# Two transformer layers on one core: attention heads turned by VectorE and exchanged through DRAM instead of transposed by TensorE, and the last product finished half by half

## The chip, the cores and the metric

The kernel runs on one core of a Trainium2 chip. The metric is the device time of one execution in microseconds (us). A difference of 0.2% (5.3 us) is about the least that a measurement of this kernel can tell from no change.

## The reference, cut to what matters

Two layers are computed one after the other on a sequence of 256 tokens and a width of 2048, all in float32.

- The first layer normalizes `x`, multiplies it with `w_in` and gets the input of two attentions of eight heads each. In MLA the queries (8 heads of 128 + 64 columns) and the keys and values (8 heads of 128 + 128 columns) come from two more products with low-rank latents; the 64 last columns of a query and one common key of 64 columns are rotated (rope). In FoX queries, keys and values (8 heads of 128) come from `w_in` directly, and a decay is added to the scores. Both are gated, then comes `w_out`, a norm and the residual.
- The second layer is a gated feed-forward block (width 5632), a mixer (three groups of four dilated attention heads of 128 columns, whose queries and keys are partly rotated, a spatial gating branch, and two gates), and a second feed-forward block. It ends with an RMS norm of the rows, times `final_norm_2`:

```python
x = x + 0.5 * swiglu(rmsnorm(x, ffn2_norm), w_gate, w_up, w_down)
return rmsnorm(x, final_norm)
```

## The kernel before, in words

**Products.** Tokens are the rows of a result: two halves of 128 tokens lie on the 128 partitions. A product streams weights in *groups* of 256 rows (two tiles of 128) by 512 columns. SyncE (SP) loads a group into one of four slots (`raw`, L322 to L334) once VectorE is done with what was there. ScalarE rounds it to `whi` (`split_hi`, L852 to L867), VectorE makes the rest `wlo = raw - whi` (`split_lo`, L1217 to L1226), both three groups ahead of TensorE (`AHEAD = 3`). TensorE multiplies (`groups`, L466 to L500): for each group 12 matmuls of 512 columns, four of `hi x whi`, four of `lo x whi`, four of `hi x wlo`. The activations are the stationary operand, transposed (`act_hi`, `act_lo`, `lat_hi`, ...). The groups that sum into one pair of accumulators (`acc`, two pairs in turn) are a *unit*: 8 groups for an input of 2048 rows, 3 for the query latent, 2 for the key-value latent, 22 for the last product of a feed-forward block. ScalarE takes half 0 of a finished unit and VectorE half 1 (`copy_out`, L936 and L1322); TensorE may start a unit only when the one before the last was taken (`acc_free`).

**Order of the work.** Everything else stands between groups, by lists written by hand. Units 3 to 5 make the queries `q`, units 6 to 9 the keys and values `kv`; VectorE rotates `q` at the first two of the latter (L1499 to L1512), its output going to `q_rope`, and the common key at the third. Then come six units of FoX queries, keys and values, four of gates and four of `w_out`. `n` counts the groups from the first FoX unit on. `MLA_STEPS` (L99) and `FOX_STEPS` (L101) say at which `n` a step of a head comes: `heads`, `scores`, `probs`, `values`. `MIX_STEPS` (L104) does the same in the mixer from its u and vs units on.

**A head before.** In the step `heads` TensorE transposes the head's queries and keys, four blocks of 128 by 128, into a PSUM bank (`job`, L502 to L511; called by `mla_step` L597, `fox_step` L615, `mix_step` L629); MLA adds two blocks of `q_rope` with every second head. ScalarE copies the bank to `qkT1` or `qkT2` (`job_out`, L954), VectorE copies the rotated part (`qrT`). In the step `scores` (L560 to L572) TensorE multiplies them: queries of the second half by 256 keys, of the first half by 128. In MLA a second pair of matmuls adds the rotated part. VectorE masks the scores and takes the row maximum, ScalarE the exponential; `probs` transposes three blocks of the probabilities, `values` multiplies with V.

**Feed-forward blocks.** Each of 11 chunks of the hidden activations is turned without TensorE: VectorE transposes it in squares of 32 by 32 (L1708, `h_turned`), and GpSimd moves it to DRAM (L428) and back in four pieces, one per 32 partitions (L431, `h_back`), by which the squares change places. Splitting it into `h_hi` and `h_lo` undoes the rest of the order (L907, L1280).

**The end.** VectorE adds the last unit to the residual (L1401) for both halves at once, takes the statistics of both (L1294), aggregates them (L1300), and with ScalarE's square root gets the row scale (L1313). Then ScalarE scales half 0 and VectorE half 1 of the four chunks of 512 columns (L1200, L1902); the gain of the last chunk is multiplied in between (L1668). SP sends each chunk, 512 KB, once both halves are ready (L395 to L399).

Of the kernel before, what the change touches and what calls it, by code (L numbers as in the profile page):

```python
# [32 lines left out]
P = 128  # L33
# [61 lines left out]
FFN1_READY = 3 + 2 * CHUNKS  # L95
FFN2_READY = FFN1_READY + FF_CHUNKS + CHUNKS + 1 + 3 + 2 * CHUNKS
# [7 lines left out]
MIX_STEPS = [(8 * h + d, step, h, g) for h in range(PER_GROUP)  # L104
             for d, step, g in ((0, "heads", 0), (1, "scores", 0), (1, "heads", 1), (2, "scores", 1),
                                (2, "heads", 2), (3, "scores", 2), (5, "probs", 0), (5, "probs", 1),
                                (6, "probs", 2), (7, "values", 0))]
# [49 lines left out]
def build(nc, x, positions, w_in, w_uq, w_ukv, b_forget, w_out, g_post, ffn1_w_gate_2, ffn1_w_up_2,  # L157
# [3 lines left out]
    with ctx:  # L161
# [36 lines left out]
        s1, pt1, qkT1 = lat[:, 0, 0:384], lat[:, 0, 384:768], lat[:, 0, 768:768 + 2 * SEQ]  # L198
        qrT, top = place_at("qrT", [P, SEQ], F32, top)
# [18 lines left out]
        rope_tmp = o_sb[:, 0, 0:4 * HEADS * ROPE // 2].rearrange("p (a h d) -> p a h d", a=4, h=HEADS)  # L218

# [21 lines left out]
        wsp_raw = u2[:, :, :].rearrange("p h n -> p (h n)")[:, 0:SG_W].rearrange("p (g s) -> p g s", g=SG_GROUPS)  # L241
        att_hi, top = place_at("att_hi", [P, PER_GROUP, SEQ], F32R, top)
# [12 lines left out]
        mix_tmp2 = pt2[:, :, :].rearrange("p g n -> p (g n)")  # L255


        h_dram = nc.dram_tensor("h_dram", (P, QUADS, TURN), F32, kind="Internal").ap()
# [16 lines left out]
        group_used = sem("group_used")  # L275
        acc_free = [sem(f"acc_free{i}") for i in range(2)]
# [4 lines left out]
        h_left, h_landed = sem("h_left"), sem("h_landed")  # L281
# [22 lines left out]
        pool_step = sem("pool_step")  # L304
        out_ready, out_sent = [sem(f"out_ready{h}") for h in range(HALVES)], sem("out_sent")
# [13 lines left out]
        def _(sp):  # L319
# [75 lines left out]
            for c in range(CHUNKS):  # L395
                for half in range(HALVES):
                    sp.wait_ge(out_ready[half], c + 1)
                sp.dma_start(out[:, c * W:(c + 1) * W].rearrange("(h p) n -> p h n", p=P),
                             xres[:, :, c * W:(c + 1) * W]).then_inc(out_sent, 16)  # L399
            sp.wait_ge(out_sent, 16 * CHUNKS)  # L400
# [6 lines left out]
        def _(pool):  # L407
# [3 lines left out]

            pool.wait_ge(forget_v, 5)
# [9 lines left out]
            blocks = h_dram.rearrange("(a j) q r -> q j a r", a=QUADS)  # L422

            def exchange_h_chunks(ready, done):

                for i in range(FF_CHUNKS):
                    pool.wait_ge(chunk_ready, ready + i + 1)
                    pool.dma_start(h_dram, h_turned[:]).then_inc(h_left, 16)  # L428
                    pool.wait_ge(h_left, 16 * (done + i + 1))
                    for quad in range(QUADS):  # L430
                        pool.dma_start(h_back[quad * QUAD:(quad + 1) * QUAD], blocks[quad]).then_inc(h_landed, 16)  # L431

            pool.wait_ge(group_used, after_first)
            exchange_h_chunks(FFN1_READY, 0)

# [4 lines left out]
            pool.dma_start(ln_b, sg_ln_b_2[:, :].partition_broadcast(P)).then_inc(ln_in, 16)  # L440
            pool.wait_ge(ln_in, 32)
# [12 lines left out]
            pool.wait_ge(group_used, after_mixer)  # L454
            exchange_h_chunks(FFN2_READY, FF_CHUNKS)
            pool.wait_ge(chunk_split, CHUNKS + FFN2_READY + FF_CHUNKS)
# [6 lines left out]
        def _(pe):  # L463
            at = Place()

            def groups(count, hi, lo, width=W, opened_by_part=False):  # L466
# [9 lines left out]
                for j in range(count):  # L476
# [9 lines left out]
                    pe.wait_ge(hi_ready, at.target("group", 1))  # L486
                    for t in range(TILES):
                        for half in range(HALVES):
                            product(hi, whi, t, half, start=first and t == 0)
# [38 lines left out]
            def h_turns():  # L528

                at.n["ready"] += 1  # L530
                at.n["chunk"] += 1

# [27 lines left out]
            def scores(terms_of):  # L560
# [4 lines left out]
                for cols, tok, keys in ((slice(0, 256), slice(P, 2 * P), slice(0, SEQ)),  # L565
                                        (slice(256, 384), slice(0, P), slice(0, P))):
                    terms = terms_of(tok, keys)
                    for n, (left, right) in enumerate(terms):
                        last = nc.tensor.matmul(s_ps[:, cols], left, right, start=(n == 0),  # L569
                                                stop=(n == len(terms) - 1), skip_group_check=True)  # L570
# [26 lines left out]
            def mla_step(step, h):  # L597
                if step == "heads":
                    job([(P, slice(half * P, half * P + P), q[:, half, h * QK:h * QK + NOPE]) for half in range(HALVES)]
                        + [(P, slice(SEQ + half * P, SEQ + half * P + P), kv[:, half, h * 2 * P:h * 2 * P + P])  # L600
                           for half in range(HALVES)])
                    if h % 2 == 0:
                        job([(P, slice(half * P, half * P + P), q_rope[:, half, h * ROPE:(h + 2) * ROPE])
                             for half in range(HALVES)])
# [10 lines left out]
            def fox_step(step, h):  # L615
                if step == "heads":
                    job([(P, slice(part * SEQ + half * P, part * SEQ + half * P + P),
                          fox[:, half, part * FOX + h * P:part * FOX + (h + 1) * P])
                         for part in range(2) for half in range(HALVES)])
                elif step == "scores":  # L620
                    transposed()
                    scores(lambda tok, keys: [(qkT1[:, tok], qkT1[:, SEQ + keys.start:SEQ + keys.stop])])
# [6 lines left out]
            def mix_step(step, h, g):  # L629
                c = (g * PER_GROUP + h) * P  # L630
                if step == "heads":
                    job([(P, slice(part * SEQ + half * P, part * SEQ + half * P + P),
                          qk2[:, half, part * ATT_W + c:part * ATT_W + c + P])
                         for part in range(2) for half in range(HALVES)])
                elif step == "scores":
                    transposed()
                    scores(lambda tok, keys: [(qkT2[:, tok], qkT2[:, SEQ + keys.start:SEQ + keys.stop])])
# [96 lines left out]
            def ffn(first_one):  # L734
# [15 lines left out]
                for i in at.loop(pe, FF_CHUNKS - 1, dict(group=2 * G_D, unit=2, chunk=1, ready=1)):  # L750
# [96 lines left out]

        @block.scalar
        def _(act):
            at = Place()  # L850

            def split_hi(n):  # L852

# [353 lines left out]
        def _(dve):  # L1207
# [545 lines left out]
            for j in groups(G_D):  # L1753
                if j == 7:
                    copy_out(qk2, slice(W, 2 * W), "mix")
# [215 lines left out]
```

## Time and profile before

| | us |
|---|---|
| median of 3 runs (2656.45 to 2657.12) | 2656.97 |
| the profiled execution's own time | 2656.65 |
| its span | 2654.8 |
| TensorE busy in the span | 2637.2 |
| VectorE busy | 1456.0 |
| ScalarE busy | 1192.1 |
| GpSimd busy | 88.8 |

The mean granted clock of TensorE is 0.998 of full speed. The span is the time from the first to the last record of the profiled execution; the execution's own time is 1.9 us longer. A busy time is the sum over an engine's instructions without overlaps; matmuls are pipelined, so the start of one to the start of the next is shorter than the duration that is printed for one.

### The profile page before, as it was taken

What the parts mean: (1) busy time and instruction counts of PE and PEld (TensorE: products, weight loads), DVE (VectorE), ACT (ScalarE), POOL (GpSimd) and SP (SyncE); (2) the same over time, 40 slices, a digit from 0 to 9 for tenths busy, and PEclk for the clock granted to TensorE, in tenths of its full rate; (3) what the DMA queues carried; (4) which work ended last, traced back from release to release, by engine and by line L of the source; (5) the groups of instructions that cost most, each with busy time, mean ns of one, the idle gap of its engine ahead of it and who ended that gap; (6) DMA issues with size and microseconds to landing.
All of it is one profiled execution on the core that took longest, in us unless ns stands there. A gap on an engine that the chain in (4) does not pass through costs nothing.

```text
span 2654.8 us, 32291 instructions
## 1 busy us (share of the span) xinstructions
PE 2637.2 (99%) x12033; PEld 2193.1 (83%) x12033; DVE 1456.0 (55%) x1594; ACT 1192.1 (45%) x1362; POOL 88.8 (3%) x137
## 2 busy tenths in 40 slices
PE   9999999999999999999999999999999999999998
PEld 8888888788888888888888888888888888888886
DVE  7755565755555555555446655555655555555554
ACT  5544554444444444444444554444444444444333
POOL 0000000000000000000000300000000000000000
PEclk9999999999999999999999999999999999999999
DMA  7655656577777775657666446665567767777654
GB/s 217 195 159 169 194 160 192 157 223 213 221 217 218 218 216 191 191 191 232 195 191 182 145 145 188 191 191 191 185 207 207 227 205 222 213 221 228 192 189 151
DMA packets 266658, 520.37 MB, mean 196 GB/s; under 512 B 19435, under 2 KB 22345, under 8 KB 266313
## 3 DMA queue, kind: packets, MB, share of 16 engines
q1 hardware_dynamic: 257456, 489.88, 61.0%
q0 software_dynamic: 8608, 29.02, 3.6%
q8 instruction: 59, 0.97, 0.1%
q10 hardware_dynamic: 504, 0.26, 0.0%
q14 instruction: 31, 0.25, 0.0%
HBM read 505.45 MB, written 13.64 MB: 196 GB/s over the span
## 4 chain that ended last, share of the span: by engine, by line
PE 99%; DVE 1%; ACT 0%; issue 0%; DVEq 0%; POOL 0%; ACTq 0%; POOLq 0%
PE acc L482 95%; PE tr L509 2%; PE s_ps L569 1%; PE o_ps L592 1%; PE s_ps L545 0%; PE tr L805 0%; DVE act_lo L1257 0%; DVE stats L1294 0%; ACT act_hi L896 0%; DVE xres L1660 0%; DVE u L1839 0%; DVE xres L1650 0%; ACT lat L958 0%; DVE xres L1902 0%; DVE xres L1401 0%
## 5 line engine op out<-in xcount | busy, mean ns | idle before, releaser
L1225 DVE TENSOR_TENSOR wlo<-raw,whi 128x1024 fp32r<-128x1024 f32 x929 | 1133.0, 1224 | 1040.6 <-ACT whi L866 1033.8
L866 ACT ACTIVATE whi<-raw 128x1024 fp32r<-128x1024 f32 x929 | 978.9, 1057 | 1121.1 <-PE acc L482 1112.8
L482 PE MATMUL acc<-whi,act_hi 128*128 128x512 f32 (+1 forms) x2560 | 693.5, 393 | 0.4 <-ACT whi L866 0.4
L482 PE MATMUL acc<-whi,act_lo 128*128 128x512 f32 (+1 forms) x2560 | 682.7, 388 | 0.0
L482 PE MATMUL acc<-wlo,act_hi 128*128 128x512 f32 (+1 forms) x2560 | 682.3, 388 | 0.0
L482 PEld LDWEIGHTS acc<-whi,act_lo 128*128 128x128 f32 x2560 | 479.6, 188 | 100.5
L482 PEld LDWEIGHTS acc<-wlo,act_hi 128*128 128x128 f32 x2560 | 479.6, 188 | 99.5
L482 PEld LDWEIGHTS acc<-whi,act_hi 128*128 128x128 f32 x2560 | 471.9, 188 | 91.7 <-issue 0.6
L482 PE MATMUL acc<-whi,h_hi 128*128 128x512 f32 x704 | 188.4, 389 | 0.0
L482 PE MATMUL acc<-wlo,h_hi 128*128 128x512 f32 x704 | 188.2, 389 | 0.0
L482 PE MATMUL acc<-whi,h_lo 128*128 128x512 f32 x704 | 188.2, 389 | 0.0
L482 PEld LDWEIGHTS acc<-whi,h_lo 128*128 128x128 f32 x704 | 132.1, 188 | 27.5
L482 PEld LDWEIGHTS acc<-wlo,h_hi 128*128 128x128 f32 x704 | 132.1, 188 | 27.5
L482 PEld LDWEIGHTS acc<-whi,h_hi 128*128 128x128 f32 x704 | 131.9, 188 | 27.2
L428 POOL DMA_DIRECT2D h_dram<-h_turned x22 | 12.4, 562 | 1476.8 <-DVE h_turned L1708 1476.8
L431 POOL DMA_DIRECT2D h_back<-h_dram x88 | 48.1, 554 | 66.8 <-DMA h_dram<-h_turned 65.4
L948 ACT ACTIVATE g_sb<-acc,rs 128x512 f32<-128x512 f32 x44 | 27.9, 686 | 33.2 <-PE acc L482 33.2
L966 ACT ACTIVATE lat<-lat,soft 128x128 f32<-128x128 f32 (+1 forms) x32 | 14.3, 449 | 57.8 <-DVE soft L1383 57.8
L1257 DVE SCALAR_TENSOR_TENSOR act_lo<-tr,gains,act_hi 128x256 fp32r<-128x256 f32 x64 | 26.6, 477 | 24.7 <-ACT act_hi L896 24.7
L958 ACT ACTIVATE lat<-tr 128x512 f32<-128x512 f32 (+1 forms) x32 | 17.4, 544 | 48.1 <-PE tr L509 48.1
L896 ACT ACTIVATE act_hi<-tr,gains 128x256 fp32r<-128x256 f32 x64 | 25.2, 474 | 30.4 <-PE tr L509 30.4
L1704 DVE SCALAR_TENSOR_TENSOR h_sb<-acc,rs,g_sb 128x512 f32<-128x512 f32 x44 | 31.0, 746 | 12.0 <-PE acc L482 12.0
(221 smaller groups left out, 1343.8 us busy)
## 6 DMA issues: line engine op xcount, KB each, us to landing
raw<-in_w_in SPq DMA_DIRECT2D x280, 512.0 KB, 3.8
raw<-in_ffn_w_gate SPq DMA_DIRECT2D x176, 512.0 KB, 4.4
raw<-in_ffn_w_up SPq DMA_DIRECT2D x176, 512.0 KB, 4.0
raw<-in_ffn_w_down SPq DMA_DIRECT2D x176, 512.0 KB, 4.7
raw<-in_w_out SPq DMA_DIRECT2D x64, 512.0 KB, 4.3
raw<-in_w_sg_out SPq DMA_DIRECT2D x24, 512.0 KB, 4.2
h_dram<-h_turned POOLq DMA_DIRECT2D x22, 512.0 KB, 3.2
h_back<-h_dram POOLq DMA_DIRECT2D x88, 128.0 KB, 5.3
```

Of the source, the lines that this page charges most:

```text
L431: pool.dma_start(h_back[quad * QUAD:(quad + 1) * QUAD], blocks[quad]).then_inc(h_landed, 16)
L482: return nc.tensor.matmul(pair[:, half, 0:width], left[:, k, half * P:(half + 1) * P], right[:, slot, t, 0:width], start=start, stop=stop, ...
L509: last = nc.tensor.transpose(tr[bank][0:rows, cols], src, ident[0:src.shape[0], 0:src.shape[0]])
L569: last = nc.tensor.matmul(s_ps[:, cols], left, right, start=(n == 0), stop=(n == len(terms) - 1), skip_group_check=True)
L592: last = nc.tensor.matmul(o_ps[:, qb * P:(qb + 1) * P], left, right, start=(n == 0), stop=(n == len(terms) - 1), skip_group_check=True)
L866: nc.scalar.activation(whi[:, slot, :, 0:width], raw[:, slot, :, 0:width], ACT.Copy).then_inc(hi_ready, 1)
L896: last = nc.scalar.activation(hi[:, tile + k, :], tr[bank][:, t * SEQ:(t + 1) * SEQ], ACT.Copy, scale=gains[:, gain + k:gain + k + 1])
L948: last = nc.scalar.activation(dest[:, half, :], a[:, half, :], func, scale=scaled(norm, half))
L958: nc.scalar.activation(dest, tr[bank][0:rows, src_cols], ACT.Copy).then_inc(tr_free[bank], 1)
L1225: nc.vector.tensor_tensor(wlo[:, slot, :, 0:width], raw[:, slot, :, 0:width], whi[:, slot, :, 0:width].bitcast(F32), ALU.subtract).then_in ...
L1257: last = nc.vector.scalar_tensor_tensor(lo[:, tile + k, :], tr[bank][:, t * SEQ:(t + 1) * SEQ], gains[:, gain + k:gain + k + 1], hi[:, til ...
L1704: last = nc.vector.scalar_tensor_tensor(h_sb[:, half, :], a[:, half, :], scaled(norm, half), g_sb[:, half, :], ALU.mult, ALU.mult)
```

## The change

- *Heads.* The step `heads` is gone from all three lists, and with it the transposes of queries and keys by TensorE and the copies `qkT1`, `qkT2`, `qrT`. VectorE turns four heads (128 x 1024 numbers) at a time in squares of 32, in two instructions (`turn_heads`), and GpSimd exchanges them through one of two DRAM buffers, as it did for the feed-forward chunks (`exchange`). There are 15 new exchanges: MLA 5 (queries of heads 0 to 3, of heads 4 to 7, rotated parts, keys 0 to 3, keys 4 to 7), FoX 4, mixer 6. The order in DRAM is such that a head lies in the landed tile at every eighth number: token, then head, then half. The scores read it there (`head_rows`).
- *Places.* MLA's turns come at the first groups of key-value units 0, 1 and 2 and of the first FoX unit; FoX's and the mixer's behind `copy_out` of the units that make queries and keys. In the mixer the rotation, two big ones before, is done there too, unit by unit. `MLA_STEPS` start at n = 8 with four groups for a head (at n = 0 with five before); both end at n = 39.
- *Waits.* VectorE waits for earlier turned tiles to have left (`turn_left`) before it overwrites them; GpSimd waits for the exchange before (`turn_landed`); TensorE waits for the exchanges that a head needs (`landed`).
- *Last group.* TensorE does half 0 of the last group, then half 1, six matmuls each, and signals after each. VectorE adds and takes the statistics of half 0 while TensorE works on half 1. The gain and the scale of the last chunk are one instruction for each half, both on VectorE; the output goes out in eight transfers of 256 KB.

```diff
-MLA_STEPS = [(5 * h + d, step, h) for h in range(HEADS)
-             for d, step in ((0, "heads"), (1, "scores"), (3, "probs"), (4, "values"))]
+EX_MLA, EX_FOX, EX_FFN1 = 0, 5, 9
+EX_MIX = EX_FFN1 + FF_CHUNKS
+EX_FFN2 = EX_MIX + 6
+MLA_STEPS = [(8 + 4 * h + d, step, h) for h in range(HEADS)
+             for d, step in ((0, "scores"), (2, "probs"), (3, "values"))]
 FOX_STEPS = [(48 + 4 * h + d, step, h) for h in range(HEADS)
-             for d, step in ((4, "values"), (0, "heads"), (1, "scores"), (3, "probs"))]
+             for d, step in ((4, "values"), (1, "scores"), (3, "probs"))]
...
+            def exchange(n, left, back):
+                pool.wait_ge(turned, n + 1)
+                pool.dma_start(turn_dram[n % 2], left.rearrange("p (q r) -> p q r", q=QUADS)).then_inc(turn_left, 16)
+                pool.wait_ge(turn_left, 16 * (n + 1))
+                if n:
+                    pool.wait_ge(turn_landed, 16 * QUADS * n)
+                for quad in range(QUADS):
+                    pool.dma_start(back[quad * QUAD:(quad + 1) * QUAD].rearrange("p (a r) -> p a r", a=QUADS),
+                                   blocks[n % 2][quad]).then_inc(turn_landed, 16)
+            for i in range(5):
+                exchange(EX_MLA + i, mla_turned[i], mla_back[i])
+            for i in range(4):
+                exchange(EX_FOX + i, fox_turned, fox_back[i])
...
 # TensorE, groups()
+                    if ends_by_half and final:
+                        pe.wait_ge(lo_ready, at.target("group", 1))
+                        for half in range(HALVES):
+                            for t in range(TILES):
+                                product(hi, whi, t, half)
+                            for t in range(TILES):
+                                product(lo, whi, t, half)
+                            for t in range(TILES):
+                                last = product(hi, wlo, t, half, stop=t == TILES - 1)
+                            last.then_inc((half_used, group_used)[half], 1)
...
+            def head_rows(back, head, tok):
+                rows = back.rearrange("p (t k h) -> p k h t", k=4, h=HALVES)[:, head]
+                if tok.stop - tok.start == P:
+                    return rows[:, tok.start // P]
+                return rows
...
             def mla_step(step, h):
-                if step == "heads":
-                    job([...])
-                elif step == "scores":
-                    transposed()
-                    scores(lambda tok, keys: [(qkT1[:, tok], qkT1[:, SEQ + keys.start:SEQ + keys.stop]),
-                                              (qrT[:, tok], (krT_odd if h % 2 else krT_even)[:, keys])])
+                if step == "scores":
+                    landed(EX_MLA + 3 + h // 4)
+                    scores(lambda tok, keys: [
+                        (head_rows(mla_back[h // 4], h % 4, tok), head_rows(mla_back[3 + h // 4], h % 4, keys)),
+                        (head_rows(mla_back[2], h // 2, tok), (krT_odd if h % 2 else krT_even)[:, keys])])
...
 # VectorE
+            def turn_heads(dest, source):
+                squares = dest.rearrange("p (q i k h) -> p h k q i", q=QUADS, k=4, h=HALVES)
+                for half in range(HALVES):
+                    last = nc.vector.transpose(squares[:, half], source[:, half].rearrange("p k (q j) -> p k q j", j=QUAD))
+                last.then_inc(turned, 1)
...
+            def add_last_residual(c, factor):
+                a, free = pair()
+                cols = slice(c * W, (c + 1) * W)
+                for half in range(HALVES):
+                    if half == 0:
+                        dve.wait_ge(half_used, 1)
+                    else:
+                        unit_ready()
+                    settled(nc.vector.scalar_tensor_tensor(xres[:, half, cols], a[:, half, :], factor, xres[:, half, cols],
+                                                           ALU.mult, ALU.add))
+                    settled(row_stats(stats, c, xres[:, half, cols], half))
+                    if half == 0:
+                        settled(aggregate("final", stats, 4, 0))
...
             for c in range(4):
                 for j in groups(KVR // P // TILES):
                     if j == 0 and c < 2:
                         if c == 0:
                             unit_out(4)
                             unit_out(5)
+                            for i in range(2):
+                                turn_heads(mla_turned[i], q[...][:, :, 4 * i:4 * i + 4, 0:NOPE])
...
+                        if c == 1:
+                            dve.wait_ge(rope_ready, 2)
+                            turn_heads(mla_turned[2], q_rope.rearrange("p a (k d) -> p a k d", d=P))
                     if j == 0 and c == 2:
+                        unit_out(6)
+                        unit_out(7)
+                        turn_keys(0)
...
             for c in range(6):
                 for j in groups(G_D):
+                    if n == 0:
+                        unit_out(8)
+                        unit_out(9)
+                        turn_keys(1)
                     attention_at(n)
                     n += 1
                     if j == 7:
+                        dve.wait_ge(turn_left, 16 * min(5, 2 * (c // 2 + 1)))
                         copy_out(fox, slice(c * W, (c + 1) * W), "pre")
+                        if c < 4:
+                            unit_out(at.n["unit"])
+                            dve.wait_ge(turn_left, 16 * (EX_FOX + c))
+                            turn_heads(fox_turned, fox[:, :, c * W:(c + 1) * W].rearrange("p a (k d) -> p a k d", d=P))
...
+            def heads_out(c):
+                copy_out(qk2, cols, "mix")
+                unit_out(at.n["unit"])
+                rotate(rows[:, :, :, 0:16], rows[:, :, :, 16:32], ...)
+                dve.wait_ge(rope_ready, rotated[0])
+                dve.wait_ge(turn_left, 16 * (EX_MIX + c))
+                turn_heads(mix_turned[:], rows)
...
+            dve.wait_ge(final_gained, CHUNKS - 1)
+            for c in range(CHUNKS - 1):
                 cols = slice(c * W, (c + 1) * W)
                 nc.vector.tensor_scalar(xres[:, 1, cols], xres[:, 1, cols], scaled("final", 1), None,
                                         ALU.mult).then_inc(out_ready[1], 1)
+            cols = slice((CHUNKS - 1) * W, CHUNKS * W)
+            for half in reversed(range(HALVES)):
+                nc.vector.scalar_tensor_tensor(xres[:, half, cols], xres[:, half, cols], scaled("final", half),
+                                               gfinal[:, cols], ALU.mult, ALU.mult).then_inc((out_last, out_ready[1])[half], 1)
```

## Rows read from the trace of the kernel before

**Rows 1.** The page: busy time of TensorE, and the chain that ended last.

```profile
PE 2637.2 (99%) x12033; PEld 2193.1 (83%) x12033; DVE 1456.0 (55%) x1594; ACT 1192.1 (45%) x1362; POOL 88.8 (3%) x137
...
PE 99%; DVE 1%; ACT 0%; issue 0%; DVEq 0%; POOL 0%; ACTq 0%; POOLq 0%
```

**Rows 2.** Waits of TensorE: total us, times, longest; the largest of four.

```profile
PE tr L509 <- DVE xres L1660: 2.7, 2, 1.7
```

**Rows 3.** Groups of instructions by form: TensorE's transposes of heads (busy us, mean ns).

```profile
L509 PE MATMUL tr<-fix,qk 128*128 128x128 f32 x48 | 7.2, 272 | 0.0
...
L509 PE MATMUL tr<-fix,o_sb 128*128 128x128 f32 x40 | 6.3, 277 | 0.4
...
L509 PE MATMUL tr<-fix,fox 128*128 128x128 f32 x32 | 4.8, 272 | 0.0
...
L509 PE MATMUL tr<-fix,q 128*128 128x128 f32 x16 | 3.0, 271 | 0.0
```

**Rows 4.** Timeline of TensorE around a FoX head and an MLA head: start us, us.

```profile
276.57 1.07 PE L482 MATMUL acc<-wlo,act_hi 128*128 128x512 f32 x4
...
278.84 1.08 PE L482 MATMUL acc<-whi,act_lo 128*128 128x512 f32 x4
279.75 1.07 PE L482 MATMUL acc<-wlo,act_hi 128*128 128x512 f32 x4
...
282.24 1.08 PE L482 MATMUL acc<-whi,act_lo 128*128 128x512 f32 x4
...
120.56 1.08 PE L482 MATMUL acc<-wlo,act_hi 128*128 128x512 f32 x4
...
123.06 1.08 PE L482 MATMUL acc<-whi,act_lo 128*128 128x512 f32 x4
```

**Rows 5.** Groups by form: the matmuls of the scores and their weight loads.

```profile
L569 PE MATMUL s_ps<-lat 128*128 128x256 f32 x32 | 9.5, 377 | 0.0
...
L569 PE MATMUL s_ps<-lat 128*128 128x128 f32 x32 | 6.1, 274 | 0.0
...
L569 PEld LDWEIGHTS s_ps<-lat 128*128 128x128 f32 x64 | 12.1, 188 | 2.1
```

**Rows 6.** VectorE's square transpose by form, and the timeline of the key-value units.

```profile
L1708 DVE STREAM_TRANSPOSE h_turned<-h_sb 128x1024 f32<-128x1024 f32 x22 | 27.4, 1245 | 0.7
...
98.43 1.23 DVE L1225 TENSOR_TENSOR wlo<-raw,whi 128x1024 fp32r<-128x1024 f32 x1 [0.97 <-ACT whi L866]
...
108.29 0.74 DVE L1326 TENSOR_SCALAR kv<-acc,rs 128x512 f32<-128x512 f32 x1
...
112.82 1.07 PE L482 MATMUL acc<-whi,lat_hi 128*128 128x512 f32 x4
```

**Rows 7.** The page, DMA issues: KB each, median us from issue to landing.

```profile
h_dram<-h_turned POOLq DMA_DIRECT2D x22, 512.0 KB, 3.2
h_back<-h_dram POOLq DMA_DIRECT2D x88, 128.0 KB, 5.3
```

**Rows 8.** The end: a group of VectorE by form, the timeline, and one window.

```profile
L1704 DVE SCALAR_TENSOR_TENSOR h_sb<-acc,rs,g_sb 128x512 f32<-128x512 f32 x44 | 31.0, 746 | 12.0 <-PE acc L482 12.0
...
2641.97 1.07 PE L482 MATMUL acc<-wlo,h_hi 128*128 128x512 f32 x4
2643.15 1.23 DVE L1401 SCALAR_TENSOR_TENSOR xres<-acc,xres 128x1024 f32<-128x1024 f32 x1 [8.57 <-PE acc L482]
2644.41 1.29 DVE L1294 BATCH_NORM_STATS2 stats<-xres 128x6 f32<-128x512 f32 x2
2645.73 0.39 DVE L1300 BATCH_NORM_AGGREGATE moments<-stats 128x2 f32<-128x24 f32 x2
...
2646.98 0.49 DVE L1902 TENSOR_SCALAR xres<-xres,rs 128x512 f32<-128x512 f32 x1
...
2647.72 3.13 SPq L398 DMA_DIRECT2D out<-xres  x4
...
2649.00:2650.00 1.00, 0.00 (x0) 0.00 (x0) 0.85 (x3) 0.53 (x1) 0.00 (x0) 0.50 0.98 381
```

More of the change, by code:

```diff
@@ L420, in _ @@
             pool.dma_start(gpost[:], g_post[:, :].partition_broadcast(P)).then_inc(gpost_in, 16)
[L422 to L434, printed above, removed]
+            flat_h = [t[:].rearrange("p q r -> p (q r)") for t in (h_turned, h_back)]
+            for i in range(FF_CHUNKS):
+                exchange(EX_FFN1 + i, *flat_h)
             pool.wait_ge(group_used, after_ffn1)
@@ L440, in _ @@
             pool.dma_start(ln_b, sg_ln_b_2[:, :].partition_broadcast(P)).then_inc(ln_in, 16)
+            for i in range(6):
+                exchange(EX_MIX + i, mix_turned[:], mix_back[i])
             pool.wait_ge(ln_in, 32)
@@ L568, in scores @@
                     for n, (left, right) in enumerate(terms):
-                        last = nc.tensor.matmul(s_ps[:, cols], left, right, start=(n == 0),
+                        out_cols = s_ps[:, cols]
+                        if len(right.shape) == 3:
+                            out_cols = out_cols.rearrange("p (h t) -> p h t", h=HALVES)
+                        last = nc.tensor.matmul(out_cols, left, right, start=(n == 0),
                                                 stop=(n == len(terms) - 1), skip_group_check=True)
@@ L615, in fox_step @@
             def fox_step(step, h):
[L616 to L622, printed above, removed]
+                if step == "scores":
+                    landed(EX_FOX + 3)
+                    scores(lambda tok, keys: [(head_rows(fox_back[h // 4], h % 4, tok),
+                                               head_rows(fox_back[2 + h // 4], h % 4, keys))])
                 elif step == "probs":
@@ L629, in mix_step @@
             def mix_step(step, h, g):
[L630 to L637, printed above, removed]
+                if step == "scores":
+                    landed(EX_MIX + 5)
+                    scores(lambda tok, keys: [(head_rows(mix_back[g], h, tok),
+                                               head_rows(mix_back[GROUPS_M + g], h, keys))])
                 elif step == "probs":
@@ L749, in ffn @@
                     pass
-                for i in at.loop(pe, FF_CHUNKS - 1, dict(group=2 * G_D, unit=2, chunk=1, ready=1)):
+                for i in at.loop(pe, FF_CHUNKS - 1, dict(group=2 * G_D, unit=2, chunk=1)):
                     for j in groups(G_D, act_hi, act_lo):
@@ L1096, in ffn @@
                     pass
-                for i in at.loop(act, FF_CHUNKS - 1, dict(group=2 * G_D, unit=2, chunk=1, ready=1, turn=1)):
+                at.n["turn"] = EX_FFN1 if first_one else EX_FFN2
+                for i in at.loop(act, FF_CHUNKS - 1, dict(group=2 * G_D, unit=2, chunk=1, turn=1)):
                     for j in groups(G_D):
@@ L1714, in ffn @@
                         gated()
-                for i in at.loop(dve, FF_CHUNKS - 1, dict(group=2 * G_D, unit=2, chunk=1, chunk_job=2, ready=1, turn=1)):
+                at.n["turn"] = EX_FFN1 if first_one else EX_FFN2
+                for i in at.loop(dve, FF_CHUNKS - 1, dict(group=2 * G_D, unit=2, chunk=1, chunk_job=2, turn=1)):
                     for j in groups(G_D):
```

179 lines of the change are left out of this document (88 added, 91 removed).

## The prediction

> **What bounds the kernel now.** I read the page first: TensorE is busy 2637.2 of 2654.8 us and makes up 99% of the chain that ended last, while VectorE has 55% and ScalarE 45% [rows 1]. Then its waits: the longest in total is 2.7 us, for two residual chunks [rows 2]. So TensorE's queue is full from start to end. An instruction taken out of it is a gain of its whole pace, as long as the two engines that prepare weights stay ahead; what the change puts on VectorE and the queues is free until it uses up that lead. Only the last 12 us belong to others: from the end of the last matmul on, VectorE, ScalarE and the output transfers follow one another [rows 8].
>
> **Transposes taken out.** The form rows show 48 transposes for the mixer, 32 for FoX, 16 for MLA's queries, as many for its keys [rows 3]. Of the 40 that read `o_sb`, 8 are of `q_rope` (four jobs of two). That is 120 in 28 jobs: 24 of four, and four in which two more are added. Their printed mean of 272 ns is latency; the pace is what counts. A set of four plain matmuls follows the one before after 279.75 - 278.84 = 0.91 us [rows 4], so a group takes 2.72 us. Around a FoX job, from the `wlo` set before to the `act_lo` set behind it are 278.84 - 276.57 = 2.27 us, where two sets take 1.82: the job of four costs 0.45 us. In MLA with six it is 123.06 - 120.56 - 1.82 = 0.68 us [rows 4]. Sum: 24 x 0.45 + 4 x 0.68 = **13.5 us** less. The copies of the banks by ScalarE and VectorE go too, at no gain: no wait of TensorE names them [rows 2].
>
> **Scores read at a stride of eight numbers.** Both operands now come from the landed tile, 32 bytes from one number to the next; the common rotated key stays packed. No row of before has a stationary or moving operand with such a step, so I bound it. A score's four passes cost 282.24 - 279.75 - 1.82 = 0.67 us in FoX [rows 4]. By form, the 256-column pass takes 377 and the 128-column pass 274 ns, so 128 columns more cost 0.103 us and a pass runs at about 0.206 or 0.103 us [rows 5]. The weight load in front of it hides behind the pass before; it takes at most the pace of a transpose, 0.45 / 4 = 0.113 us. Lower bound: nothing, since these passes take a column in 0.80 ns where the fp32r matmuls take 512 in 0.91 / 4 = 0.227 us, 0.44 ns each [rows 4, 5]. The fetch of a number therefore has almost twice the time that packed operands need. Upper bound, every strided read at half the pace: 28 pairs of head operands (8 MLA, 8 FoX, 12 mixer) x 2 x (0.206 + 0.103) = 17.3 us, and for MLA's rotated term, where only the load is strided, its 0.226 us stands against the passes of 0.206 and 0.103: 8 x 2 x (0.02 + 0.123) = 2.3 us. Together 19.6 us. Below nothing is excluded, for the matmuls stay the same in number and columns. I take **0**, because the nearest rows are those of the same passes, which leave this spare time per number; the upper end is kept.
>
> The Trainium skill speaks against the change here. "Advanced Engine Details and Errata", section "SBUF Cachelines", says that lines have 16 bytes, that at least two hits on one are needed to cover the memory's latency, and that a different line for each access costs a penalty. By that rule each number of these operands is such a miss, and the sum would come out near the upper bound. No row of before shows it either way.
>
> **VectorE and its lead.** A square transpose of 1024 numbers takes 1.245 us [rows 6]; in two halves I put 1.35 us. Fifteen are 20 us of an engine with 1200 us to spare, but they fall in bursts. In the FoX and mixer units a burst (copy, rotation, turn) is 2 to 4 us in 21.8, against a lead of three groups, 8.2 us: nothing. The tight place is the key-value units, of two groups (5.4 us) each. There VectorE takes its half of key-value unit 1 at 108.29, done at 109.03, and TensorE needs that accumulator at 112.82 [rows 6]: 3.8 us of room. Three turns are put ahead of it, 4.05 us, of which VectorE's idle gaps between 98.43 and 108.29 swallow about 0.3 to 0.6. I take **0.3 us** more. Queued behind these turns on VectorE are `wlo` of the next groups (they keep about 2 us) and SP's loads. Upper bound, if writing at a stride doubles the turns: 3 x 2.7 - 3.8 - 0.6 = 3.7 us there, and about 4.5 us by the next unit, whose copy has four turns ahead of it. Below nothing: excluded, since no work of VectorE's that TensorE waits for is removed here.
>
> **Exchanges.** One takes 3.2 us out and 5.3 back [rows 7], 8.5 if nothing overlaps. The first turn of MLA ends near 98.43 + 1.23 + 1.35 = 101.0 us; four exchanges in a row end by 135. The first FoX unit starts 5.9 us behind 112.82, at 118.7, and head 0's scores stand eight groups later, at 140.5: 5 us of room. VectorE's wait for the fifth to have left, at the end of the same unit, comes due when it has (135 + 3.2). FoX's and the mixer's have 22 us each and whole units before the scores. Cost 0; upper bound, if the exchanges take 11.5 us each under the weights' own traffic, 6 us. GpSimd has nothing else queued behind them that is due.
>
> **The end.** Half 0 of the last group is done six matmuls early, 6 x 0.227 = 1.36 us. VectorE's add can start at 2643.15 - 1.36 = 2641.8. With 0.746 us for an add of 512 numbers, 1.29 / 2 for its statistics, 0.39 / 2 for the aggregate and 0.03 between them [rows 8], half 0 is through at 2643.5 and half 1 at 2645.2, where both were at 2646.12: 0.9 us. The first transfer then leaves after a single scale of 0.49 instead of 0.74 us behind 2646.98: some 0.1 more. The rest is bandwidth: 2.1 MB at 381 GB/s are 5.5 us [rows 8], which hides the last chunk's gain and scale. In sum **1.0 us** less; 1.3 at most, and nothing if eight issues at the pace of four in 3.13 us become the limit.
>
> **Sum**, against the profiled execution's own 2656.65: -13.5 - 1.0 + 0.3 gives 2642.45. The median is 0.3 above that execution, so 2642.8 us, 0.5% faster.
>
> **Rivals.**
> - *Strided reads at half pace on TensorE* (the rule above, as a mechanism). For it: the packed fp32r operands show four neighbouring numbers in 1.8 ns [rows 4], while these need a number from a new place every 0.8 ns [rows 5]. Against: these passes have twice the time per number. 2642.8 + 19.6 = 2662.4, up to 2667 with VectorE's writes slowed too. The other side: it decides once the strided passes cost above 0.5 us more per head pair (14.2 / 28), for then the whole gain is eaten.
> - *Only the loads slowed, or all by a part.* 36 terms (28 and MLA's 8) x 2 x 0.143 = 10.3 us: 2653, between 2647 and 2658.
> - *The key-value stage stalls*: VectorE behind its turns, or head 0 waiting for its exchange, 3 to 6 us: 2646 to 2649. For it: 3.8 us of room against 4.05. Against: the lead of three groups comes back within a FoX unit.
> - *The transposes were hidden*, so nothing is gained: 2656. Against it stands the pace around a job [rows 4]; 1%.
>
> **How the numbers follow.** Forecast 0.62; stride in full 0.12; stride in part 0.14; stall 0.11; nothing gained 0.01. The forecast's own range is 2640.5 (jobs at 0.48 us and an end 1.3 us shorter) to 2646. The range that should hold 8 in 10 takes in stalls and partial stride: 2640.5 to 2657. Against the 5.3 us (0.2%) that a measurement can tell, faster (below 2651.7) are the forecast, the stall and half of the partial case: 0.80. Within it the rest of that case, nothing gained and a little of the full one: 0.10. Slower: 0.10.
>
> **What would show it.** After: TensorE has no `tr<-qk`, `tr<-fox`, `tr<-q` or `tr<-kv` rows; the span from the `wlo` set before a FoX score to the `act_lo` set behind stays 2.49 us (3.1 with the full stride); weight loads of `s_ps` stay at 188 ns; VectorE's transposes of 512 numbers take about 0.7 us (1.2 if strided writes cost); TensorE's waits name neither `kv` copies nor landings above 0.5 us; the aggregate of half 1 ends 2.1 us behind the last matmul. A pace of the scores above 3 us, or waits above 3 us between 100 and 145 us, would make the forecast wrong.

## The result and the profile after

The changed kernel takes 2669.13 us (median of 5 runs, 2668.63 to 2669.55), the kernel before 2656.97: a ratio of 1.0045, with a 95% interval of 1.0034 to 1.0057. It is 12 us slower, where 14 us less were forecast. The profiled execution took 2668.63 us, its span 2666.8.

The page of the changed kernel, busy time and chain:

```profile
PE 2645.7 (99%) x11913; PEld 2196.3 (82%) x11913; DVE 1484.8 (56%) x1644; ACT 1177.7 (44%) x1333; POOL 130.8 (5%) x212
...
PE 98%; DVE 1%; DMA 0%; issue 0%; ACT 0%; SPq 0%; DVEq 0%; ACTq 0%
```

TensorE has 120 matmuls fewer than in [rows 1], as the change says (12033 to 11913), and is busy 8.5 us longer. So the loss is on TensorE itself: fewer instructions, some of them longer. The chain is still its own. Its form rows say which, here for the FoX queries and keys (busy us, mean ns), with the weight loads (PEld):

```profile
L627 PE MATMUL s_ps<-fox,late 128*128 128x256 f32 x8 | 4.4, 634 | 0.0
...
L627 PE MATMUL s_ps<-fox,late 128*128 128x128 f32 x8 | 2.6, 414 | 0.0
...
L627 PEld LDWEIGHTS s_ps<-fox,late 128*128 128x128 f32 x16 | 4.7, 316 | 1.2 <-issue 0.6
```

The same passes were 377 and 274 ns, their loads 188 [rows 5]. From 128 to 256 columns a pass now grows by 634 - 414 = 220 ns, where it grew by 103: about 0.44 and 0.22 us for a pass, twice as much and a little more. The timeline of TensorE gives the price of a score as the prediction read it, here around a FoX head and around the first MLA head (start us, us):

```profile
285.77 1.08 PE L514 MATMUL acc<-wlo,act_hi 128*128 128x512 f32 x4
286.68 1.56 PE L627 MATMUL s_ps<-fox,late 128*128 128x256 f32 x4
287.87 1.29 PE L514 MATMUL acc<-whi,act_hi 128*128 128x512 f32 x4
289.00 1.08 PE L514 MATMUL acc<-whi,act_lo 128*128 128x512 f32 x4
...
146.47 1.08 PE L514 MATMUL acc<-wlo,act_hi 128*128 128x512 f32 x4
...
150.53 1.08 PE L514 MATMUL acc<-whi,act_lo 128*128 128x512 f32 x4
```

FoX: 289.00 - 285.77 - 1.82 = 1.41 us instead of 0.67 [rows 4], 0.74 more; a mixer score, read in the same way at 1459.44 to 1462.68, costs 1.42. MLA: 150.53 - 146.47 - 1.82 = 2.24 us. In the kernel before, the same span around MLA's first score (123.97 to 127.13 in its timeline) was 3.16, so 1.34: 0.89 more. Together 20 x 0.74 + 8 x 0.89 = 21.9 us.

The second loss stands in the waits of TensorE (total us, times, longest) and in VectorE's form row of a turn:

```profile
PE tr L554 <- DVE xres L1742: 2.8, 2, 1.7
PE acc L514 <- ACT whi L911: 1.4, 1, 1.4
PE acc L514 <- DVE kv L1376: 1.4, 1, 1.4
PE tr L554 <- DVE u L1924: 1.1, 2, 0.5
PE s_ps L600 <- POOL ones L430: 1.0, 1, 1.0
PE tr L554 <- DVE lat L1404: 1.0, 1, 1.0
PE acc L514 <- issue: 0.5, 1, 0.5
...
L1331 DVE STREAM_TRANSPOSE mix_turned<-qk 128x512 f32<-128x512 f32 x12 | 13.0, 1162 | 0.2
```

They sum to 9.2 us; before they were 5.2, with the largest in [rows 2]. The waits for a copy of `kv` (1.4) and for the rotated key in `lat` (1.0) are new, and so is the 0.5 put down to `issue`; the one for weights has grown from 0.4 to 1.4. With 0.1 more for `xres` that makes 4.0 us. A turn of 512 numbers takes 1.16 us, so two halves take 2.3, not 1.35. The timeline of VectorE in the key-value units, against [rows 6], shows the queue that this makes; the last line is TensorE's:

```profile
99.62 4.14 DVE L1331 STREAM_TRANSPOSE fox<-q 128x512 f32<-128x512 f32 x4
...
110.90 2.17 DVE L1331 STREAM_TRANSPOSE fox<-o_sb 128x512 f32<-128x512 f32 x2
112.90 1.23 DVE L1265 TENSOR_TENSOR wlo<-raw,whi 128x1024 fp32r<-128x1024 f32 x1
114.04 0.74 DVE L1376 TENSOR_SCALAR kv<-acc,rs 128x512 f32<-128x512 f32 x1
...
114.83 1.21 PE L514 MATMUL acc<-whi,lat_hi 128*128 128x512 f32 x4 [1.41 <-DVE kv L1376]
```

The copy that ended at 109.03 now ends at 114.78, and TensorE, which wants that accumulator at 112.36 + 0.91 = 113.3, starts at 114.83.

The end of the changed kernel, in the timeline:

```profile
2655.05 0.61 PE L514 MATMUL acc<-wlo,h_hi 128*128 128x512 f32 x2
2655.07 0.69 DVE L1340 BATCH_NORM_STATS2 stats<-xres 128x6 f32<-128x512 f32 x1
2655.80 0.26 DVE L1344 BATCH_NORM_AGGREGATE moments<-stats 128x2 f32<-128x24 f32 x1
2656.09 0.69 DVE L1467 SCALAR_TENSOR_TENSOR xres<-acc,xres 128x512 f32<-128x512 f32 x1
2656.82 0.69 DVE L1340 BATCH_NORM_STATS2 stats<-xres 128x6 f32<-128x512 f32 x1
2657.55 0.26 DVE L1344 BATCH_NORM_AGGREGATE moments<-stats 128x2 f32<-128x24 f32 x1
...
2658.67 1.28 DVE L1985 TENSOR_SCALAR xres<-xres,rs 128x512 f32<-128x512 f32 x3
2659.19 4.05 SPq L420 DMA_DIRECT2D out<-xres  x8
```

The last matmul ends at 2655.66. The aggregates are done 2.15 us later, where that was 3.08 [rows 8], and the first scale starts 3.0 us later instead of 3.94. From the first transfer to the end of the span it is 7.6 us, though, where it was 7.1. The end is 11.1 instead of 11.8 us: 0.6 less.

The account closes: -13.5 for the transposes, +21.9 for the scores, +4.0 for waits, -0.6 at the end are +11.8; the span grew by 12.0. The 13.5 is still the forecast's own figure here; the run without strides, below, gives it a measurement.

### The profile page after: what moved, and what is told of

It is laid out like the page before. It is cut to its first block, busy times and chain, and to the rows that moved or that the text cites. A ratio compares the mean times of both kernels' runs of the same rounds, so it can differ in the third digit from the quotient of the medians.

```text
span 2666.8 us, 32167 instructions
## 1 busy us (share of the span) xinstructions
PE 2645.7 (99%) x11913; PEld 2196.3 (82%) x11913; DVE 1484.8 (56%) x1644; ACT 1177.7 (44%) x1333; POOL 130.8 (5%) x212
## 4 chain that ended last, share of the span: by engine, by line
PE 98%; DVE 1%; DMA 0%; issue 0%; ACT 0%; SPq 0%; DVEq 0%; ACTq 0%
PE acc L514 94%; PE s_ps L627 2%; PE tr L554 1%; PE o_ps L650 1%; DVE fox L1331 0%; DMA raw<-in_w_in 0%; PE tr L849 0%; DVE wlo L1265 0%; DVE act_lo L1297 0%; DVE stats L1340 0%; DVE xres L1742 0%; ACT whi L911 0%; DVE u L1924 0%; DVE xres L1732 0%; ACT lat L1002 0%
## 5 line engine op out<-in xcount | busy, mean ns | idle before, releaser
L439 POOL DMA_DIRECT2D turn_dram<-h_turned x22 | 12.3, 561 | 1481.0 <-DVE h_turned L1790 1481.0
L444 POOL DMA_DIRECT2D h_back<-turn_dram x88 | 48.1, 553 | 65.9 <-DMA turn_dram<-h_turned 64.7
L514 PE MATMUL acc<-whi,merged_hi 128*128 128x512 f32 x128 | 34.6, 392 | 0.0
```

The lines of the kernel that those rows point to most:

```text
L444: pool.dma_start(back[quad * QUAD:(quad + 1) * QUAD].rearrange("p (a r) -> p a r", a=QUADS), blocks[n % 2][quad]).then_inc(turn_landed, 16)
L514: return nc.tensor.matmul(pair[:, half, 0:width], left[:, k, half * P:(half + 1) * P], right[:, slot, t, 0:width], start=start, stop=stop, ...
```

## The experiments

My theory at this point: TensorE and VectorE pay for every number of a strided operand; nothing else is wrong with the change. The rivals were traffic of the exchanges (for the waits), conflicts over the landed tiles (for the scores), and the weight loads rather than the passes. The kernel before, run beside these, took 2658.8 (one run) and 2657.2 and 2657.1 us (medians of 7 and 9). Of the variants only the last three (the queries copied, and the two that vary the end) ran more than once. A single run can lie a microsecond or two off, as the 2658.8 shows, so where less than that is at stake the timelines and form rows decide, not the time.

**VectorE writes in runs of 32.** The order of the tokens is then another than the scores take them for, with the same work.

```diff
-                squares = dest.rearrange("p (q i k h) -> p h k q i", q=QUADS, k=4, h=HALVES)
+                squares = dest.rearrange("p (q k h i) -> p h k q i", q=QUADS, k=4, h=HALVES)
```

> The changed kernel with one edit: VectorE writes its turned squares in runs of 32 neighbouring numbers instead of at every eighth (the tokens then come in another order, same work for everybody else). Theory: writing at a stride of 32 bytes doubled the 512-number transpose (1.15 us instead of about 0.7) and that burst made the waits of TensorE for key-value copies, rotated keys and weights between 110 and 126 us, about 3.8 us in all. Expected: transposes of 0.7 us, those waits below 1 us, the time 2669.1 - 3.5 = about 2665.5. Rival: the waits come from the exchanges' traffic, which delays weights; then transposes get faster but the time stays within 1 us of 2669.

Measured: 2665.45 us. Waits of TensorE and the form row of a turn:

```profile
PE tr L554 <- DVE xres L1742: 2.8, 2, 1.7
PE tr L554 <- DVE u L1924: 1.1, 2, 0.5
PE s_ps L600 <- POOL ones L430: 1.0, 1, 1.0
PE acc L514 <- ACT whi L911: 0.6, 1, 0.6
PE acc L514 <- issue: 0.5, 1, 0.5
...
L1331 DVE STREAM_TRANSPOSE mix_turned<-qk 128x512 f32<-128x512 f32 x12 | 7.8, 690 | 0.2
```

The turn falls from 1.16 to 0.69 us and with it the waits from 9.2 to 6.0 us, while the exchanges are the same. Of the 4.0 us that the change added to the waits, 3.2 were VectorE's burst of strided writes, not traffic.

**TensorE reads neighbouring numbers.** The scores are then of other numbers than a head's; shapes, waits and transfers stay.

```diff
-                rows = back.rearrange("p (t k h) -> p k h t", k=4, h=HALVES)[:, head]
-                if tok.stop - tok.start == P:
-                    return rows[:, tok.start // P]
-                return rows
+                return back[:, head * SEQ + tok.start:head * SEQ + tok.stop]
```

> The changed kernel, but the scores read both operands from neighbouring numbers of the landed tile (other numbers than the head's, same shapes, waits and traffic). Theory: strided reads by TensorE cost 0.74 us for a FoX or mixer score and 0.89 us for an MLA score, 8 x 0.89 + 20 x 0.74 = 21.9 us. Expected: pace of a FoX score back to 0.67 us, weight loads of the scores back to 188 ns, 2669.1 - 21.9 = about 2647. Rival: the scores are slow because the landed tiles share memory with tiles that VectorE, ScalarE or the queues write at the same time; then packed reads stay slow and the time above 2665.

Measured: 2647.25 us, 21.9 less than the changed kernel; loads at 188 to 190 ns, the FoX score at 281.68 - 279.20 - 1.82 = 0.66 us. The 256-column pass is back from 634 ns:

```profile
L624 PE MATMUL s_ps<-fox,late 128*128 128x256 f32 x8 | 2.4, 377 | 0.0
```

The tiles lie where they lay, and the waits stay at 9.3 us. So neither the place of the tiles nor what else touches them slows the scores; how they are read is the whole of it.

**Only the queries packed.** The stationary operand is read as above, the keys at every eighth number.

```diff
-                        (head_rows(mla_back[h // 4], h % 4, tok), head_rows(mla_back[3 + h // 4], h % 4, keys)),
+                        (query_rows(mla_back[h // 4], h % 4, tok), head_rows(mla_back[3 + h // 4], h % 4, keys)),
...
```

> The changed kernel, but only the stationary operand (queries) is read packed; the keys that stream are still at every eighth number. Theory: the streaming pass is what costs (0.44 and 0.22 us for 256 and 128 columns), the strided load of 0.22 us hides behind it except where MLA's rotated term streams packed keys. Expected: loads of about 188 ns, FoX score still 1.3 to 1.4 us, gain 1 to 2 us, about 2667. Rival: the load sets the pace; then the gain is 10 to 20 us, 2650 to 2659.

Measured: 2667.33 us, and a FoX score of 288.01 - 284.80 - 1.82 = 1.39 us. The loads are short again (187 to 210 ns), the passes are not:

```profile
L631 PE MATMUL s_ps<-fox,late 128*128 128x256 f32 x8 | 4.3, 630 | 0.0
```

It helps by 1.8 us only. The first MLA score, from 146.84 to 150.71 in its timeline, costs 2.05 us instead of 2.24, and 8 x 0.19 + 20 x 0.02 = 1.9. The strided loads were hidden behind the longer passes, except in MLA's rotated term.

**Only the keys packed.** The keys are turned and read in runs of 32, in the right order; the queries stay at every eighth. This is the whole computation.

```diff
+            def key_rows(back, head, keys):
+                rows = back.rearrange("p (a k h i) -> p k h a i", a=QUADS, k=4, h=HALVES)[:, head]
+                if keys.stop - keys.start == P:
+                    return rows[:, keys.start // P]
+                return rows
...
+                if keys:
+                    squares = dest.rearrange("p (q k h i) -> p h k q i", q=QUADS, k=4, h=HALVES)
...
```

> [...] The result is the whole computation. Theory: passes return to 0.206 and 0.103 us, the strided loads of about 0.22 us then set the pace, a FoX score costs about 0.9 us instead of 1.41: 28 x 0.5 = 14 us less, and the keys' turns are faster too (1 to 2 us): about 2654. Rival (loads dominate already): a FoX score stays above 1.3 us and the time above 2664.

Measured: 2654.46 us. The timeline of TensorE at a FoX score, and the load's form row:

```profile
282.56 1.08 PE L514 MATMUL acc<-wlo,act_hi 128*128 128x512 f32 x4
283.47 0.99 PE L636 MATMUL s_ps<-fox,late 128*128 128x256 f32 x4
284.22 1.17 PE L514 MATMUL acc<-whi,act_hi 128*128 128x512 f32 x4
285.23 1.07 PE L514 MATMUL acc<-whi,act_lo 128*128 128x512 f32 x4
...
L636 PEld LDWEIGHTS s_ps<-fox,late 128*128 128x128 f32 x16 | 4.1, 328 | 0.2
```

A score costs 285.23 - 282.56 - 1.82 = 0.85 us. Its four strided loads start at 283.24, 283.48, 283.70 and 283.94, and the packed load behind them at 284.18: they stand 0.22 to 0.24 us apart, whether 256 or 128 columns stream, and that is the pace of a strided load. So packing the streaming operand alone wins back some three quarters of the loss (0.56 of 0.74 us a score), and the load, hidden until then, is what remains. MLA's score falls to 1.82 us (146.56 to 150.20), and 20 x 0.56 + 8 x 0.42 = 14.6 of the 14.7 us that were measured. The faster turns of the keys gave little: the waits fall from 9.2 to 8.8 us, where 1 to 2 us were expected. Whether runs of 32 stream at the full pace can't be seen here, behind the loads; the kernel with the queries copied shows it.

**The step varied.** Both operands at every second, third and fourth number of the tile, again other numbers than a head's. The edit of the pe_packed kernel, with n = 2, 3, 4:

```diff
+                return back[:, 0:256*n].rearrange("p (t s) -> p s t", s=n)[:, head % n, tok]
```

> The changed kernel, but both operands of the head scores are read at every second number (8 bytes apart) of the landed tile; other numbers than the head's, same shapes. Theory A (what costs is a new line of 16 bytes for each number; two numbers of a line are enough): a FoX score is back at 0.67 us, weight loads at 188 ns, time near the 2647 us of packed reads. Theory B (the cost grows with the step): between packed and every eighth, a FoX score of about 0.8 to 1.0 us and a time of 2650 to 2657.

> The changed kernel, both operands of the head scores at every third number (12 bytes apart). Theory A (a line of 16 bytes is fetched anew for each number that lies in another line, three of four here): a FoX score between, 1.1 to 1.3 us, about 2660 to 2665. Theory B (the step alone decides, below 16 bytes is free): 0.67 us and 2647.

> The changed kernel, but both operands of the head scores are read at every fourth number (16 bytes apart). Theory A (a new line of 16 bytes each): the full cost of every eighth, a FoX score of 1.41 us, loads of about 320 ns, about 2669 us. Theory B (grows with the step): a FoX score of 0.9 to 1.2 us and 2655 to 2662 us.

Measured, with pe_packed as step 1 and the changed kernel as step 8 (the score from the timeline as above, load and 256-column pass from the form rows):

| step | bytes | time, us | FoX score, us | load, ns | pass, ns |
|---|---|---|---|---|---|
| 1 | 4 | 2647.25 | 0.66 | 188 | 377 |
| 2 | 8 | 2647.43 | 0.70 | 194 | 387 |
| 3 | 12 | 2659.83 | 1.05 | 252 | 504 |
| 4 | 16 | 2668.55 | 1.38 | 310 | 629 |
| 8 | 32 | 2669.13 | 1.41 | 316 | 634 |

The form rows of the kernels with steps 2, 3 and 4:

```profile
L624 PE MATMUL s_ps<-fox,late 128*128 128x256 f32 x8 | 2.5, 387 | 0.0
L624 PEld LDWEIGHTS s_ps<-fox,late 128*128 128x128 f32 x16 | 3.1, 194 | 0.6
```

```profile
L624 PE MATMUL s_ps<-fox,late 128*128 128x256 f32 x8 | 3.4, 504 | 0.0
L624 PEld LDWEIGHTS s_ps<-fox,late 128*128 128x128 f32 x16 | 3.9, 252 | 0.8
```

```profile
L624 PE MATMUL s_ps<-fox,late 128*128 128x256 f32 x8 | 4.3, 629 | 0.0
L624 PEld LDWEIGHTS s_ps<-fox,late 128*128 128x128 f32 x16 | 4.6, 310 | 1.3
```

Step 2 is almost free, 4 and 8 cost the same, 3 lies half way (1.05 us a score, a little below the 1.1 to 1.3 of its theory A). A cost that grew with the step (theory B of steps 2 and 4) would not be flat from 4 to 8, and one with an edge (theory B of step 3) would not lie half way. It goes by how many new 16-byte pieces are touched per number: 1/2, 3/4, 1, 1. At one piece each, 128 columns take 0.22 us, 1.7 ns a piece; at three quarters that makes 0.33 us for 256 columns against 0.21 packed, 0.12 more, and the pass grew by 0.127. For step 2 the same working gives 128 pieces, 0.22 us, 0.01 above packed, and the pass grew by 0.010. The Trainium skill, in "Advanced Engine Details and Errata", section "SBUF Cachelines", speaks of lines of 16 bytes, of which each needs at least two hits to cover the memory's latency. The runs agree: at step 2 every line is hit twice and the pass takes 387 ns against 377, at steps 4 and 8 once and it takes 629 and 634. That latency is the cause was not tested; the count of pieces was.

**The change without strides.** pe_packed and dve_packed in one kernel.

> The changed kernel with VectorE writing its squares in runs of 32 and TensorE reading neighbouring numbers for both operands (other numbers than the head's, same shapes, exchanges and waits). Theory: this is the change without any stride, and its time is what the forecast put down for it, transposes -13.5, end -0.6 to -1.0, stall +0.3: 2643 to 2644. Rival (a part of the 12 us is neither stride nor stall): above 2646.

Measured: 2643.66 us, 0.9 from the forecast of 2642.8. This is what the prediction had priced. The waits are 6.1 us, 0.9 above before, none of them for a copy of `kv`; the end is 11.1 us, 0.6 below. The span is 13.0 us shorter than before, so 13.0 - 0.6 + 0.9 = 13.3 us are left for the transposes, where 13.5 were forecast.

**A version that computes the whole.** After the exchange with such turns the tokens of a head come in runs of 32, four for each half. The keys are streamed in these runs; the queries, the stationary operand, are read from one packed row. ScalarE copies a head's queries (and MLA's rotated ones) into it one group ahead, 256 numbers a partition, in two places in turn; for MLA and FoX they lie in a free part of the tile `lat`, by which the profile names them. Everything is turned in runs of 32.

```diff
-                squares = dest.rearrange("p (q i k h) -> p h k q i", q=QUADS, k=4, h=HALVES)
+                squares = dest.rearrange("p (q k h i) -> p h k q i", q=QUADS, k=4, h=HALVES)
...
+            def pack(n, tile, back, head, ex, rotated=None):
+                act.wait_ge(turn_landed, 16 * QUADS * (ex + 1))
+                if n >= 2:
+                    act.wait_ge(scores_done, n - 1 + (n - 2 >= HEADS))
...
+                copy(tile[:, n % 2 * SEQ:(n % 2 + 1) * SEQ], back, head).then_inc(q_packed, 1)
...
+                    pe.wait_ge(q_packed, HEADS + h + 1)
+                    scores(lambda tok, keys: [(packed(h, tok),
```

> The whole computation without strides on TensorE: queries and keys are turned and landed in runs of 32; keys stream in such runs; ScalarE copies each head's queries (and MLA's rotated ones) from the landed tile to neighbouring numbers one group ahead of the score, two buffers in turn. Theory: a score is back at 0.67 us, the transposes stay away, ScalarE has room for 32 copies of 0.43 us (it loses 28 of 0.6 us against before): 2643 to 2645, 0.5% faster than before. Rival: runs of 32 stream slower than packed, or the copies delay the weights' rounding: a score of 0.75 us and more or new waits, 2647 to 2652.

Measured: 2644.19 us (4 runs, 2643.73 to 2644.59), a ratio of 0.9951 to the kernel before, interval 0.9934 to 0.9968: faster than before and than the changed kernel. The form rows of ScalarE's copies, of the loads and of the 256-column passes, and the timeline at a FoX score:

```profile
L1025 ACT ACTIVATE lat<-late 128x256 f32<-128x256 f32 x12 | 4.9, 408 | 0.0
...
L636 PEld LDWEIGHTS s_ps<-fox,lat 128*128 128x128 f32 x32 | 6.0, 188 | 1.1
L636 PE MATMUL s_ps<-fox,lat 128*128 128x256 f32 x16 | 4.7, 377 | 0.0
...
276.13 1.07 PE L516 MATMUL acc<-wlo,act_hi 128*128 128x512 f32 x4
277.04 0.81 PE L636 MATMUL s_ps<-fox,lat 128*128 128x256 f32 x4
277.61 1.17 PE L516 MATMUL acc<-whi,act_hi 128*128 128x512 f32 x4
278.63 1.08 PE L516 MATMUL acc<-whi,act_lo 128*128 128x512 f32 x4
```

The score costs 278.63 - 276.13 - 1.82 = 0.68 us, and the passes take 377 ns: runs of 32 stream as fast as packed numbers. No wait of TensorE names the copies, and the waits sum to 6.4 us against 6.1 without the copies.

**The end alone**, on queries_copied: once with the end of the kernel before, once with the new end but four transfers. The edit of the second:

```diff
                         sp.wait_ge(out_ready[half], c + 1)
-                    sp.dma_start(out[half * P:(half + 1) * P, c * W:(c + 1) * W],
-                                 xres[:, half, c * W:(c + 1) * W]).then_inc(out_sent, 16)
+                sp.dma_start(out[:, c * W:(c + 1) * W].rearrange("(h p) n -> p h n", p=P),
+                             xres[:, :, c * W:(c + 1) * W]).then_inc(out_sent, 16)
...
```

> queries_copied with the end of the kernel before: both halves of the last group together, add and statistics of both halves, the gain apart, four output transfers of 512 KB. Theory: the new end is worth 0.6 us (0.9 us earlier row scale, 0.5 us given back by the eight transfers): 0.6 us above queries_copied's 2644.2, 2644.8; its profile shows 11.75 us from the end of the last matmul to the end of the span. Rival: the new end is worth nothing or less, 2644.2 or below.

> queries_copied with the new end but the output in four transfers of 512 KB, each after both halves. Theory (eight issues cost time): transfers as long as before, 7.1 instead of 7.6 us from the first issue to the end of the span, with the first issue 0.2 us later: 0.3 us less than queries_copied, 2643.9. Rival (the eight transfers are not the cause): the same 7.6 us, 2644.4.

Measured: 2644.96 us (2644.49 to 2647.6) with the old end, 2644.50 (2644.12 to 2644.61) with four transfers, against 2644.19. Their ratios to the kernel before, 0.9957 (0.9944 to 0.9971) and 0.9953 (0.9939 to 0.9967), overlap with that of queries_copied, so the times don't settle a few tenths; that of four transfers lies 0.3 above queries_copied, not 0.3 below as expected. The timelines of one execution each do for their part of the span: 11.8 us from the end of the last matmul to the end of the span with the old end, 11.1 with eight transfers, 10.8 with four (6.95 from the first issue on instead of 7.6). By these the new end is worth 0.6 to 0.7 us, and it would be worth 0.3 to 0.4 more with four transfers instead of eight. The eight issues take 4.05 us and the four 2.89; why the data end later was not tried further.

## Why the prediction was wrong

The forecast was 2642.8 us, in a range to 2657; the time was 2669.1. What failed is one choice: of the two bounds for **scores read at a stride of eight numbers**, 0 and 19.6 us, I took 0 "because the nearest rows are those of the same passes, which leave this spare time per number". The rows showed 0.44 ns per number for packed fp32r and 0.80 ns for these passes, and I counted room in numbers. The unit is the 16-byte piece: packed fp32r touches one every 1.77 ns, and the strided pass wanted one every 0.80 ns. Counted so, the same rows had shown a rate less than half of what was wanted. They did not show it to be a limit; the runs did, with 1.7 ns a piece and 21.9 us gone once the reads were packed. The rule of the Trainium skill stood beside the sum and had the right unit; the trace had no strided operand to set against it, and the rival that it spoke for should have carried more than 0.12.

- *Transposes*, -13.5: right, with 13.3 left for them in all_packed.
- *Strided scores*: the upper bound of 19.6 us was nearly exact; 21.9 measured. Half the pace was a little too fast: the passes take 0.44 and 0.22 us where twice 0.206 and 0.103 were put in.
- *VectorE's lead*: taken as 0.3 us, bound 3.7 to 4.5 if strided writes doubled the turns. They went from 0.69 to 1.16 us and TensorE waited 4.0 us more; dve_packed takes back 3.2 us of waits and 3.7 of time. The place, the key-value units, was the forecast one. With turns of 0.69 us no wait names a copy of `kv`, but the waits still grow by 0.9, not 0.3.
- *Exchanges*: they come 6.5 to 10 us apart, not 8.5 at most (issues at 102.09, 108.57, 116.72, 125.92 and 135.97 us), within the bound of 11.5. No wait of TensorE names a landing.
- *The end*: 1.0 us was forecast, 0.6 came. The row scale is 0.9 us earlier as worked out; the eight transfers, put down as a bound only, gave 0.5 back (7.6 us from the first issue to the end instead of 7.1), and why is open.
- *The rival*: strided reads at half pace on TensorE, with VectorE's writes slowed too, was written down with 2667 us. It is what happened, 2 us above its figure, so the mechanism was known beforehand and its chance was put too low.

## What to carry to other kernels

Before a transpose is replaced by a layout in which an operand comes at a step, count 16-byte pieces, not numbers: for 4-byte numbers a step of 2 was free here, 3 cost half and 4 and 8 the whole, on TensorE's streaming operand and its weight load. VectorE's writes were tried at 8 only, and cost 1.7 times as much. Let an engine with spare time undo the odd order (here ScalarE, 0.41 us a head), and let the engine that bounds the kernel read runs of neighbouring numbers. Where the unknown cost of one access pattern is as large as the whole gain, the sign of the change hangs on it.

## What the runs showed of the hardware that I had not expected

- A step of 16 bytes is as dear as one of 32 (2668.55 and 2669.13 us), and one of 8 as cheap as none (2647.43 and 2647.25). The prediction's sum counted with no such edge.
- A strided weight load of 0.22 to 0.24 us hides behind strided passes (stationary_packed gains 1.8 us only) and sets the pace once the passes are packed (keys_packed, 0.85 us for a score against 0.68). The two losses don't add.
- VectorE's square transpose of 512 numbers takes 0.69 us when it writes runs of 32 and 1.16 when it writes at every eighth; the reading side was packed in both.
